# Block 1's sub-norm root taken in two parts, its first mixed tile turned earlier, and block 2's context rows loaded during the attention

## The reference

```
a = diff_attention(dq, dk, dv, lam, pos)
a = a * lax.rsqrt(jnp.mean(a * a, axis=-1, keepdims=True) + SUBLN_EPS) * g_subln.astype(jnp.float32) * (1.0 - lambda_init)
...
mixed = jnp.concatenate([a, bo, co], axis=-1) * jax.nn.silu(gate.astype(jnp.float32))
out = jnp.einsum('bse,ed->bsd', mixed.astype(x.dtype), w_out)
return layer_norm(DEEPNORM_ALPHA * x + out, ln_g, ln_b)
```

```
h = _modulate(_rmsnorm(x, g_attn[i]), sh_a, sc_a)
hc = _modulate(_rmsnorm(xc, g_attn[i]), shc_a, scc_a)
q, k, v = _split_qkv(h, w_qkv[i])
qc, kc, vc = _split_qkv(hc, w_qkv[i])
```

## Time and profile before

| | |
|---|---|
| median of 3 runs | 2954.38 us |
| all runs | 2951.1, 2954.95, 2954.38 us |
| the profiled execution's own time | 2950.66 us |
| its span in the profile | 2949.0 us |
| TensorE busy (PE) | 2803.7 us, 95% |
| VectorE (DVE), ScalarE (ACT), GpSimd (POOL) busy | 39%, 26%, 11% |
| mean granted TensorE clock | 0.981 of full speed |

### The profile page before, as it was taken

How to read it: one execution, slowest core, us unless ns; L and a number is a source line. 1 busy time by engine, 2 the same in 40 slices (tenths; PEclk the granted TensorE clock), 3 DMA queues, 4 the chain that set the end, 5 groups by cost and what they waited for, 6 DMA issues and landing times. The chain is left out here.

```text
span 2949.0 us, 65190 instructions
## 1 busy us (share of the span) xinstructions
PE 2803.7 (95%) x27105; PEld 1659.6 (56%) x27109; DVE 1144.1 (39%) x2781; ACT 761.1 (26%) x1599; POOL 323.3 (11%) x584
## 2 busy tenths in 40 slices
PE   8999999999889999999999999989899999999996
PEld 4444655444554457645666666644576566666663
DVE  2572653472654245545211122253443611112214
ACT  1111531110542147621111111143674111111111
POOL 3000430000440000011010000020000100000011
PEclk9999999999989999999999999999999999999998
DMA  7212653211653100146999999962002599999994
GB/s 272 70 57 86 231 161 97 78 66 57 238 186 137 57 1 2 57 166 222 397 401 400 397 398 401 396 235 99 1 2 108 210 384 400 399 399 401 399 400 169
DMA packets 155504, 636.94 MB, mean 216 GB/s; under 512 B 19744, under 2 KB 24352, under 8 KB 138960
## 3 DMA queue, kind: packets, MB, share of 16 engines
q1 hardware_dynamic: 114624, 517.59, 45.5%
q0 software_dynamic: 40720, 117.18, 11.7%
HBM read 582.70 MB, written 52.00 MB: 215 GB/s over the span
## 5 line engine op out<-in xcount | busy, mean ns | idle before, releaser
L1128 PE MATMUL PJ<-WR,XT 128*128 128x512 f32 (+2 forms) x1152 | 475.2, 568 | 5.7 <-ACT XT L140 2.9
L140 ACT ACTIVATE PT<-TR 128x512 f32<-128x512 f32 (+3 forms) x384 | 177.8, 493 | 880.6 <-PE TR L1357 736.9
L1128 PEld LDWEIGHTS PJ<-WR,XT 128*128 128x128 f32 x1152 | 215.6, 191 | 243.9 <-issue 215.7
L140 DVE TENSOR_TENSOR PR<-G 128x384 f32<-128x384 f32 x64 | 35.8, 559 | 737.9 <-ACT G L140 737.5
L1086 PE MATMUL PJ<-WR,XT 128*128 128x512 f32 x576 | 260.1, 608 | 1.8 <-ACT XT L140 1.4
L1337 PE MATMUL SC<-QK,XT 128*64 128x256 f32 x2112 | 244.1, 385 | 0.0
L140 DVE TENSOR_REDUCE SM<-SC 128x1 f32<-128x768 f32 (+6 forms) x208 | 173.7, 835 | 152.6 <-PE SC L1106 143.8
L1288 PE MATMUL PJ<-WR,XT 128*128 128x512 f32 x512 | 227.1, 596 | 1.0 <-issue 1.0
L1337 PE MATMUL SC<-WR,XT 128*64 128x256 f32 x1984 | 226.2, 381 | 0.0
L1337 PEld LDWEIGHTS SC<-QK,XT 128*64 128x64 f32 x2112 | 150.2, 138 | 86.3 <-issue 16.0
L140 ACT ACTIVATE PR<-SC,SM 128x256 f32<-128x256 f32 (+5 forms) x288 | 187.6, 669 | 41.4 <-DVE SM L140 27.2
(11 more groups left out here) (253 smaller groups left out, 3344.0 us busy)
## 6 DMA issues: line engine op xcount, KB each, us to landing
QK<-in_w_gate_dram SPq DMA_DIRECT2D x34, 2048.0 KB, 9.5
WR<-in_w_down_dram SPq DMA_DIRECT2D x34, 2048.0 KB, 15.8
QK<-in_w_up_dram SPq DMA_DIRECT2D x32, 2048.0 KB, 14.4
WR<-in_w_up_dram SPq DMA_DIRECT2D x32, 2048.0 KB, 14.4
WR<-in_w_gate_dram SPq DMA_DIRECT2D x30, 2048.0 KB, 9.5
QK<-in_w_down_dram SPq DMA_DIRECT2D x30, 2048.0 KB, 15.9
WR<-in_w_ada_dram SPq DMA_DIRECT2D x24, 2048.0 KB, 8.1
WR<-in_w_in_dram SPq DMA_DIRECT2D x14, 2048.0 KB, 7.9
```

What stands on the lines that cost most here:

```text
L140: return lambda *a, **k: Signal(make(*a, **k), self)
L1128: m = mm(bank[:, 0:n], XT1[:, c, s.t * P:(s.t + 1) * P], w[:, c, 0:n], start=c == 0, stop=c == DC - 1)
```

## The change

- The sub-norm is cut in two parts: `roots(0)` (12 sums, tiles 0 to 2) is put into turn 31 of the attention, ahead of the last `ada` step and behind the last exponentials. `roots(1)` (4 sums, tile 3) stands behind the attention.
- Tile 0 is scaled in turn 32, tile 1 behind the attention, tiles 2 and 3 after `roots(1)`. The turn of tile 0 is put into turn 34, behind the last sums.
- In layer 2, the context rows have buffers of their own, `BC[:, 2D:3D]` and `STG[:, 0:D]`, and their own semaphores. GpSimd issues their loads in the attention, in the `ada` step 1, behind the bias loads for step 3.
- The first context tile is turned behind `wout_first` of tile 0, the second behind `wout` of tile 0 and ahead of `wout_first` of tile 1. `load2` stands behind `wout` of tile 0. The x rows of tiles 0 and 1 no longer wait for `norm0`.

```diff
-        attend(unit_list, extra={i: ada(j) for j, i in enumerate(ADA_AT)})
-        add("subln", l=l)
+        def roots(part, l=l):
+            add("sub_roots", l=l, part=part, roots=((0, 3), (3, 4))[part])
+
+        def scale(part, tiles, first, l=l):
+            add("sub_scale", l=l, part=part, roots=((0, 3), (3, 4))[part] if first else None, tiles=tiles)
...
+        extra = {i: ada(j) for j, i in enumerate(ADA_AT)}
+
+        def roots_and_ada(go=extra[31]):
+            roots(0)
+            go()
+
+        extra[31] = roots_and_ada
+        extra[32] = lambda: scale(0, (0,), True)
+        extra[34] = lambda: mixturn(0)
+        attend(unit_list, extra=extra)
+        scale(0, (1,), False)
         wo = [weight("w_out", l=l, half=h) for h in range(2)]
         bc = take("bc")[0]
         add("load_bc", bc=bc, what="ln", l=l)
...
-        mixturn(0)
         fins = []
         if l == DEPTH - 1:
             for t in range(XT_TILES, XT_TILES + CTX_TILES):
                 ctx_fins.append(add("norm0", l=0, t=t, fin=take("fin")[0], ctx=True))
-            add("load2", l=0)
+        roots(1)
+        scale(1, (2, 3), True)
         for t in range(XT_TILES):
+            if t == 1 and ctx_fins:
+                xt_ready[ctx_fins[1].t] = add("fin_turn", f=ctx_fins[1], tr=take("tr", 2)).tr[-1]
             pjs = take("pj", 2)
             add("wout_first", l=l, t=t, u=wo[0], pj=pjs, src_tr=turned[t])
             if t + 1 < XT_TILES:
                 mixturn(t + 1)
-            behind = [fins[t - 1]] if t else ctx_fins
+            behind = [fins[t - 1]] if t else ctx_fins[0:1]
...
+            if l == DEPTH - 1 and t == 0:
+                add("load2", l=0)
...
         def x_rows_of(f):
+            if f.kind == "norm0":
+                return BC[:, 2 * D:3 * D] if f.t == XT_TILES else STG[:, 0:D]
...
-                elif s.kind == "subln":
-                    act.wait_ge(sub_in, s.l + 1)
-                    A(RS, SS, ACT.Sqrt).then_inc(sub_out, 1)
+                elif s.kind == "sub_roots":
+                    act.wait_ge(sub_in, 2 * s.l + s.part + 1)
+                    heads = slice(4 * s.roots[0], 4 * s.roots[1])
+                    A(RS[:, heads], SS[:, heads], ACT.Sqrt).then_inc(sub_out, 1)
...
             def x_slot_free(f):
 
                 prev = by_fin.get(f.fin - 2)
-                if prev is None:
+                if prev is None or prev.kind == "norm0":
                     return
...
+                    if s.j == 1 and s.l == DEPTH - 1:
+                        pool.wait_ge(tr_full, staged_last + 1)
+                        for f in ctx_rows:
+                            load_fin(f)
```

More of the change, by code:

```diff
@@ L153, in __init__ @@
                  tr_before=None, src_tr=None, after=None, tiles=None, turns=None, slot=None, loads=None, prev=None,
-                 cols=None, half=None, base=None, order=None, xe0=None, keys=None, full=None, inner=None, near=None, moe=None, late=False):
+                 cols=None, half=None, base=None, order=None, xe0=None, keys=None, full=None, inner=None, near=None, moe=None, late=False,
+                 part=None, roots=None):
         self.kind, self.l, self.t, self.h, self.j, self.c, self.e = kind, l, t, h, j, c, e
@@ L168, in __init__ @@
         self.near, self.moe, self.late = near, moe, late
+        self.part, self.roots = part, roots
 def make_plan(until=99):
@@ L369, in ada, with mixturn @@
             return go
-        attend(unit_list, extra={i: ada(j) for j, i in enumerate(ADA_AT)})
-        add("subln", l=l)
+        turned = {}
+        def mixturn(t, l=l):
+            turned[t] = add("mix_turn", t=t, l=l, tr=take("tr", 2)).tr[-1]
+        def roots(part, l=l):
[11 more added lines that the diff above has]
+        scale(0, (1,), False)
         wo = [weight("w_out", l=l, half=h) for h in range(2)]
@@ L375, in make_plan @@
         add("load_bc", bc=bc, what="ln", l=l)
-        turned = {}
-        def mixturn(t, l=l):
-            turned[t] = add("mix_turn", t=t, l=l, tr=take("tr", 2)).tr[-1]
-        mixturn(0)
         fins = []
@@ L583, in finish_plan @@
         k = s.fin % 2
-        s.far = s.kind == "combine" and (s.t >= 2 if s.last else s.t == 2)
+        s.far = s.kind == "norm0" or s.kind == "combine" and (s.t >= 2 if s.last else s.t == 2)
         count["far"][k] += s.far
@@ L1612, in _ @@
                     k = s.fin % 2
-                    act.wait_ge(xs_loaded[k], 16 * s.load)
+                    act.wait_ge(far_loaded[k], 16 * s.far_load)
                     act.wait_ge(rms_in, s.fusedn)
-                    A(JUNK, XS[:, k * D:(k + 1) * D], ACT.Square, accum_out=SQS[:, k:k + 1]).then_inc(act_done, 1)
+                    A(JUNK, x_rows_of(s), ACT.Square, accum_out=SQS[:, k:k + 1]).then_inc(act_done, 1)
                     act.wait_ge(act_done, s.normn)
@@ L1846, in finish_fused @@
                     dve.wait_ge(tr_full, prev.turned + 1)
-                TS(normed_rows(s), XS[:, k * D:(k + 1) * D], RSTD[:, k:k + 1], None, ALU.mult).then_inc(fin_done, 1)
+                TS(normed_rows(s), x_rows_of(s), RSTD[:, k:k + 1], None, ALU.mult).then_inc(fin_done, 1)
             PARTNERS = [(32 * f + 16 * k, 32 * f + 16 - 16 * k) for f in range(2) for k in range(2)]
@@ L2087, in _ @@
                         v.increment(dve, ada_ready, 1)
[L2088 to L2091, removed]
+                elif s.kind == "sub_roots":
+                    heads = slice(4 * s.roots[0], 4 * s.roots[1])
+                    dve.wait_ge(square_done, 16 * s.l + 4 * s.roots[1])
+                    now(TS(SS[:, heads], SS[:, heads], 1.0 / P, EPS1, ALU.mult, ALU.add))
                     v.increment(dve, sub_in, 1)
[L2093 to L2096, removed]
+                elif s.kind == "sub_scale":
+                    if s.roots:
+                        lam_init = 0.8 - 0.6 * math.exp(-0.3 * s.l)
+                        heads = slice(4 * s.roots[0], 4 * s.roots[1])
+                        dve.wait_ge(sub_out, 2 * s.l + s.part + 1)
+                        now(reciprocal(RS[:, heads], RS[:, heads]))
+                        now(TS(RS[:, heads], RS[:, heads], 1.0 - lam_init, None, ALU.mult))
+                    for t in s.tiles:
                         for h in range(4):
@@ L2125, in _ @@
                 elif s.kind == "norm0":
-                    dve.wait_ge(xs_loaded[s.fin % 2], 16 * s.load)
+                    dve.wait_ge(far_loaded[s.fin % 2], 16 * s.far_load)
                     v.increment(dve, rms_in, 1)
@@ L2633, in _ @@
             adas = [s for s in steps if s.kind == "ada"]
+            ctx_rows = [s for s in steps if s.kind == "norm0"]
+            staged_last = [s for s in steps if s.kind == "stage_turn"][-1].tr[-1]
             def quarter(q, o):
```

## The result

| | before | change |
|---|---|---|
| median | 2952.3 us (5 runs, 2945.94 to 2954.95) | 2930.62 us (5 runs, 2927.03 to 2933.28) |
| ratio, 95% interval | | 0.9927 [0.9911, 0.9942] |
| profiled execution, its span | 2950.66, 2949.0 us | 2928.32, 2926.6 us |
| mean granted TensorE clock | 0.981 | 0.987 |

A forecast was written before the change was run, and what follows sets the result against it. TensorE, busy 95% of the span, was taken as the bound. Terms 7.8 + 13.2 - 0.3 = 20.7 us off 2950.66 gave 2930.0, plus 3.7 for a median: 2933.7 us, range 2926.7 to 2941.4.

The forecast's parts named there:

- The first boundary: End of block 1's first attention, up to the output projections: less idle and a higher clock gain 7.8 us.
- Steps 1 and 2: First boundary: early root costs the path nothing; tile 0's scaling ends 0.23 after the last sums, idle 5.16 becomes about 0.3.
- Step 3: First boundary: work moved behind tile 0's scaling idles TensorE about 1.0 more; projection starts 5.5 us earlier.
- Step 4: First boundary: TensorE keeps the high clock, so the projection's first half takes 7.03 instead of 9.72, 2.7 less.
- Step 5: First boundary: tile 0's x rows land late, at 413.9, holding a bank TensorE wants for tile 1; some 0.4 lost.
- The second boundary: End of block 1's second attention: the same steps plus context rows loaded early gain 13.2 us.
- The even odds of the clock: Second boundary, around tile 2's turn: idle pieces may lower the clock, even odds of 1.7 us; 0.8 taken off.
- The early loads: Two 512 KB loads on GpSimd's queue in the second attention: store 2 lands 2 to 4 late, cost 0.3 us.
- The rule on the table load: At each early root: the skill's drain of about 1.38 us per table switch would make the gain 1 to 2 smaller.
- the clock still falls at the first boundary: Rival: clock falls after the new short holes at both boundaries; gain 15.3, time 2939.1 us, chance 0.17.
- the chain of loads only moves the wait: Rival, both boundaries: TensorE only reaches GpSimd's chain sooner, waiting for x rows and modulation vectors; 2953 us, chance 0.06.
- The slower end by missed bias rows: Rival, second attention: 1 MB on GpSimd's queue makes every later bias load miss its step; 2960 us, chance 0.03.

The follow-up runs named there:

- Products of nothing: The kernel before plus five unused products on TensorE between the last sums and tile 0's turn, both layers: ratio 0.9988 to the kernel before.
- root only: The change with the root early, but tile 0 scaled and turned behind the attention: ratio 0.9967 to the kernel before.
- late loads: The change with its two context loads issued in `ada` step 8 instead of 1: ratio 0.9935 to the kernel before.
- the turn alone: The change with its context part undone, early root in two parts and early turn kept: ratio 0.9973 to the kernel before.
- neither part alone: The change with its context part undone (0.9973), and the change with its root part and early turn undone (0.9984), each against the kernel before.
- both edits: The change with x rows ahead of layer-norm rows and second context tile's copies ahead of tile 0's norm steps: 0.9929, again 0.9930 to before.

## Why the prediction was right

**The first boundary, 7.8 forecast, 7.0 measured.**
- Steps 1 and 2 held. The table load began 2.89 ahead of the last sums (397.33 - 394.44 in ScalarE's timeline; 395.41 - 392.5 = 2.91 by the forecast) and the sums weren't held. Tile 0 was ready 0.06 behind them, not 0.23, and its turn followed the sums after 0.12 us, at the second boundary after 0.11.
- Step 3 held: 1.03 of idle behind the turn (about 1.0), the projection 4.43 behind the start of the sums (4.34), 5.4 earlier for 5.5.
- Step 4 held, 2.6 for 2.7. Products of nothing give the same 7.13, so it is the idle stretch that drops the clock, and nothing in the data or the weights.
- Step 5 was mis-sized: 0.4 for the late x rows. It is 1.06 (27.07 less 26.01), with 0.82 of it idle. The loads issue at the same distance from the sums as before (11.9 and 12.0 us), and the first landed 7.2 behind its issue instead of 6.5. That landing is no constant: in five traces the idle is 0 to 1.06.

**The second boundary, 13.2 forecast, 12.1 measured.** Up to tile 1's second half the gain was 13.3 (46.65 from S2 before, 33.38 in the change), with 14.0 forecast. The first square of the context began 5.63 behind the start of the last sums (5.64), the hole directly ahead of the first context turn was 0.42, and ScalarE's queue held tile 2's turn as described: 1.28 and 0.68 of idle where 1.1 and 0.9 were expected (874.0 to 875.1, and 876.5). The 0.7 that was missed lies there: the turn's two parts came 0.3 later, and the turn of tile 0's rows behind them took 1.69, where it takes 1.23 with the clock held (root only and late loads). The even odds of the clock came out against the change: 15.06 for 13.90, so 1.2 where 0.8 was taken off. With the 0.46 of that turn the fall cost 1.6, close to the full 1.7 that was put on it.

**The early loads, -0.3 forecast, nothing measured.** Store 2 landed 2.6 later (1.07 of issue and 1.47 of landing), inside the 2 to 4 forecast, and the idle of 3.01 took it up. That the chain does pass a delay on where no such idle is, the late loads show: 1.8 us.

**The rule on the table load.** From the end of the exponentials to the root are 1.49 us (838.77 less 836.01 + 1.27): 0.19 of idle, the load of 1.28, and 0.02. The Trainium skill (ScalarE: Activation LUTs, What ACT_TABLE_LOAD costs) puts about 1.38 of drain beside a load of 1.28 in every switch, 2.66 in all. The trace of the change disagrees with that again.

**The number.** The mechanisms held, and the closeness of the number is in part luck. The sum was 2930.0 for a profiled execution, which took 2928.32; the boundaries give 19.1 of the 22.4, where 20.7 was forecast, and clock in code that was not moved gives the 3 us that the forecast does not have. The median was forecast 3.7 above the sum, since the median shown stood so far above its own profiled execution. Over five runs before's median stands 1.6 above (2952.3 to 2950.66) and the change's 2.3 (2930.62 to 2928.32), hence less than 2933.7. One sum of the range was off: clock and chain both against it leave 15.3 - 3.7 = 11.6, not 13, which would put the upper end 1.4 us higher.

**The rivals.** That the clock still falls at the first boundary is what the root alone does (9.04 us behind a hole of 3.26); with the turn moved as well it doesn't (7.13). That the chain of loads only moves the wait is what the turn alone does (11.05); the context's own buffers prevent it. The slower end by missed bias rows did not begin: VectorE's last wait for one is 0.61, before 1.12.

## What to carry to other kernels

A tail between two phases is worth more than its idle time where the clock falls in it; measure how long the same records take behind the hole and elsewhere, and aim for holes that the clock was seen to bear, here about a microsecond, in one piece. When one wait is removed, ask what the next consumer is pinned to: here the early turn gave nothing at the second boundary until the context rows no longer hung on another chain, and neither part alone would have told of the 7.7 us that they have together. Look for the next queue that holds copies behind work that is itself waiting, and don't expect the last 3 us to be seen in whole times that scatter as these do.

## What the runs showed of the hardware

- Whether the clock falls is not settled by the idle time alone. Holes in one piece of up to 1.39 us never brought it down in these stretches, and it fell behind every one of 3.17 and more (behind the 3.17, with 1.33 of idle following, the first eight transposes still took 1.06). In the mixture stretch one hole of 2.06 stands in all twelve traces, and the next six records of 512 columns took 4.12 to 5.47 us, where twelve of them take 5.40 a little later: the clock fell each time, and what differs is how soon it came back. Around tile 2's turn, with 1.21 to 1.28 and then 0.68 of idle and four transposes between, the 32 records behind took 15.06, 14.72, 14.95 and 14.23 us in four traces and 13.90 in two, with the same instructions.
- Two loads of 512 KB on GpSimd's queue, issued right ahead, delayed the landing of the small stores behind them by 1.5 us (3.56 of idle for 2.09).
- The same TensorE instructions differ between executions by several us: S lies between 395.2 and 400.7 over twelve traces (397.3 and 395.6 in the change's two), and S to S2 is 439.6 in one trace with both edits and 444.0 in the other.
